# The opening of a two-block transformer forward pass: modulation panels taken in pairs, and the first activations sent through the first up panel chunk by chunk

## What is computed

```python
def modulate(x, shift, scale):
    return x * (1.0 + scale) + shift

def half_ffn(h, shift, scale, gate, wg, wu, wd):
    return h + 0.5 * gate * swiglu(modulate(rms_norm(h), shift, scale), wg, wu, wd)

h = x + grid_pos_embed(n_lat)          # latent tokens, 256 x 1024
hc = ctx                               # context tokens, 256 x 1024
m  = split(silu(c) @ mod_w + mod_b, 9)         # nine vectors of 1024
mc = split(silu(c_ctx) @ mod_w + mod_b, 9)
h  = half_ffn(h,  m[0],  m[1],  m[2],  ffn_w_gate, ffn_w_up, ffn_w_down)
hc = half_ffn(hc, mc[0], mc[1], mc[2], ffn_w_gate, ffn_w_up, ffn_w_down)
```

## Time and profile before

| | us |
|---|---|
| time, median of 3 runs (lowest to highest) | 1908.37 (1902.5 to 1908.42) |
| the profiled execution's own time | 1909.65 |
| its span | 1907.8 |
| TensorE busy in the span | 1850.8 (97%) |
| VectorE busy | 1193.7 (63%) |
| ScalarE busy | 449.5 (24%) |
| GpSimd busy | 531.7 (28%) |
| mean granted TensorE clock | 0.989 of full |

### The profile page before, as it was taken

One profiled execution on the slowest core, in us unless ns is written; L12 is line 12 of the kernel. 1 busy time (PEld: TensorE's weight loads), 2 busy tenths in 40 slices (PEclk: granted clock), 3 DMA queues, 4 the chain that ended last, 5 costly groups with the idle time before them and its releaser, 6 DMA issues.

```text
span 1907.8 us, 32733 instructions
## 1 busy us (share of the span) xinstructions
PE 1850.8 (97%) x13326; PEld 1700.6 (89%) x13326; DVE 1193.7 (63%) x1548; ACT 449.5 (24%) x748; POOL 531.7 (28%) x613
## 2 busy tenths in 40 slices
PE   5999999999999999999999999999999999999999
PEld 2777777887999979999999998999999999899999
DVE  6654543325257987545576976875557796787554
ACT  3100000103121221211135544321112555431110
POOL 1112122121235304343340002553334000244342
PEclk8999999999999999999989999999999999999999
DMA  9325665321333425355544433455454433344552
GB/s 371 119 99 221 259 237 233 133 108 45 111 126 118 160 74 191 145 183 189 179 155 155 155 133 122 144 185 190 177 181 174 169 139 133 133 155 177 185 190 88
DMA packets 44914, 307.35 MB, mean 161 GB/s; under 512 B 5376, under 2 KB 5888, under 8 KB 8320
## 3 DMA queue, kind: packets, MB, share of 16 engines
q1 hardware_dynamic: 40912, 292.66, 42.1%
q10 hardware_dynamic: 3888, 13.03, 1.9%
HBM read 302.53 MB, written 3.15 MB: 160 GB/s over the span
## 4 chain that ended last, share of the span: by engine, by line
PE 87%; DVE 7%; DMA 2%; issue 2%; ACT 1%; SPq 0%; POOL 0%; DVEq 0%; ACTq 0%; POOLq 0%
PE ps L2025 53%; PE ps L2054 23%; DVE wlo L728 2%; DMA landing<-in_stream 1%; DMA ws<-in_stream 1%; PE ps L2536 1%; PE ps L2183 1%; PE ps L2560 1%; PE ps L2546 1%; DVE xlo L795 1%; PE ps L2444 1%; PE ps L2452 1%; PE ps L2510 1%; PE ps L2594 1%; PE ps L2078 1%
## 5 line engine op out<-in xcount | busy, mean ns | idle before, releaser
L728 DVE TENSOR_TENSOR wlo<-landing,whi 128x1024 fp32r<-128x1024 f32 x484 | 610.8, 1297 | 263.7 <-PE ps L2054 171.2
L650 POOL TENSOR_TENSOR whi<-landing,ones 128x16 fp32r<-128x16 f32 x198 | 74.5, 376 | 1355.5 <-PE ps L2025 895.9
L2025 PE MATMUL ps<-xhi,whi 128*128 128x256 f32 (+1 forms) x2368 | 365.8, 306 | 6.4 <-ACT xhi L1691 3.2
L2025 PE MATMUL ps<-xlo,whi 128*128 128x256 f32 (+1 forms) x2368 | 352.4, 301 | 1.1 <-DVE xlo L795 1.1
L2025 PEld LDWEIGHTS ps<-xhi,whi 128*128 128x128 f32 x2368 | 322.6, 193 | 30.1 <-issue 11.8
L2025 PE MATMUL ps<-xhi,wlo 128*128 128x256 f32 (+1 forms) x2368 | 347.0, 299 | 0.5 <-DVE wlo L728 0.5
L2025 PEld LDWEIGHTS ps<-xlo,whi 128*128 128x128 f32 x2368 | 320.9, 193 | 16.4 <-DVE xlo L795 1.5
L2025 PEld LDWEIGHTS ps<-xhi,wlo 128*128 128x128 f32 x2368 | 317.3, 191 | 14.5 <-DVE wlo L728 0.9
L653 POOL TENSOR_SCALAR whi<-landing 128x1024 fp32r<-128x1024 f32 x198 | 230.3, 1163 | 0.0
L652 POOL TENSOR_SCALAR whi<-landing 128x1008 fp32r<-128x1008 f32 x198 | 228.3, 1153 | 0.0
L2054 PE MATMUL ps<-xhi,whi 128*128 128x256 f32 (+1 forms) x1152 | 167.8, 298 | 5.9 <-issue 5.0
(11 more groups left out here) (284 smaller groups left out, 1736.6 us busy)
## 6 DMA issues: line engine op xcount, KB each, us to landing
landing<-in_stream SPq DMA_DIRECT2D x250, 1024.0 KB, 4.8
ws<-in_stream SPq DMA_DIRECT2D x28, 1024.0 KB, 5.0
spectra<-big ACTq DMA_DIRECT2D x8, 256.0 KB, 4.3
ws<-spectra ACTq DMA_DIRECT2D x2, 1024.0 KB, 5.4
ws<-in_tabs ACTq DMA_DIRECT2D x1, 1280.0 KB, 6.1
h<-in_xT ACTq DMA_DIRECT2D x1, 1024.0 KB, 6.3
ws<-in_ctxT ACTq DMA_DIRECT2D x1, 1024.0 KB, 15.2
ws<-in_window ACTq DMA_DIRECT2D x1, 1024.0 KB, 13.6
```

The source lines that it names most:

```text
L650: pool.tensor_tensor(hi[:, 0:FIRST], panel[:, 0:FIRST], ones[:, 0:FIRST], ALU.mult)
L728: ins = v.tensor_tensor(wlo[:, s % 2, c], landing[:, s, c], whi[:, s % 2, c].bitcast(F32), ALU.subtract)
L2025: ins = mm(out, a, b, start=first and opens and k == ks[0], stop=last and k == ks[-1], skip_group_check=True)
```

## The change

The eight lead panels are reordered into four pairs, (0, 4), (1, 5), (2, 6), (3, 7): shift and scale of the same two chunks. Each pair gets its own copy, turn and addition (`pair_copy`, `turn_pair`, `add_pair`), and the addition writes the scale columns straight into `gains`. `first_parts(p)` on VectorE and `first_highs(p)` on ScalarE then make the high and low parts of chunks 2p and 2p+1, and `first_pass(p, ...)` on TensorE runs them through the first up panel, between the lead products. The first up panel gets a buffer of its own (`first_up`) and is loaded behind the second lead panel. The first lead panel is loaded in two halves. The folding of the squares on VectorE is gone, and TensorE adds all eight chunks of squares itself (eight products of 128 x 256 for each token set in place of one). `ctxT` is loaded before `mats`, and `low(G_UP1)`, which stood ahead of `add_mod(0)`, stands behind the last `first_parts`. The core of the diff:

```diff
+        N_PAIR = N_LEAD // 2
+        LEAD = tuple(p + UNROLL * q for p in range(N_PAIR) for q in range(2))
+        first_up = flatc(35, PANEL // T)
+        up0_in = sem("up0_in")
...
-            for g in range(SLOTS):
-                sp.dma_start(landing[:, g], stream[g]).then_inc(landed[g], 16)
+            half = PANEL // 2
+            for n in range(2):
+                c = slice(n * half, (n + 1) * half)
+                sp.dma_start(landing[:, 0, c], stream[0][:, c]).then_inc(landed[0], 16)
+            for g in range(1, SLOTS):
+                sp.dma_start(landing[:, g], stream[LEAD[g]]).then_inc(landed[g], 16)
+                if g == 1:
+                    sp.dma_start(first_up, stream[G_UP1 + N_REST]).then_inc(up0_in, 16)
...
-            for g in (*range(SLOTS, N_LEAD - 1), G_UP1, N_LEAD - 1, *range(G_UP1 + 1, first_rest)):
+            for g in (*range(SLOTS, N_LEAD), *range(G_UP1 + 1, first_rest)):
...
+            def add_pair(p):
+                dve.wait_ge(mod_turned, p + 1)
+                turned = ps[:, 4, 0:16].rearrange("p (c n b) -> p n c b", n=UNROLL, b=2)
...
+                v.tensor_tensor(mcol[:, 2 * p:2 * p + 2, :], turned[:, 0], bias(0), ALU.add).then_inc(mod_added, 1)
+                v.scalar_tensor_tensor(gains[:, 0:2, 2 * p:2 * p + 2].rearrange("p b c -> p c b"), turned[:, 1], 1.0, bias(1),
+                                       ALU.add, ALU.add).then_inc(cols_set, 1)
+            for p in range(N_PAIR):
+                add_pair(p)
+                first_parts(p)
+                if p == 1:
+                    sine_argument(1)
             low(G_UP1, G_UP1 % SLOTS)
-            add_mod(0)
-            add_mod(1)
...
+            pair_copy(0)
+            sine(0)
             log_exp()
             norm_rms(0, 2)
             norm_rms(1, 3)
+            pair_copy(1)
+            first_highs(0)
+            pair_copy(2)
+            first_highs(1)
             sine(1)
-            mod_copy(0)
-            mod_copy(1)
+            pair_copy(3)
+            first_highs(2)
             filter_loads()
-            act.wait_ge(mod_added, 1 + 2)
+            act.wait_ge(mod_added, 1 + N_PAIR)
+            first_highs(3)
...
             def lead(n):
-                pe.wait_ge(landed[n % SLOTS], (n // SLOTS + 1) * 16)
-                mod_product(n, landing[:, n % SLOTS]).then_inc(panel_used, 1)
+                s = n % SLOTS
+                pe.wait_ge(landed[s], (n // SLOTS + (1 if s else 2)) * 16)
+                if n >= 4 and n % 2 == 0:
+                    pe.wait_ge(mod_copied, n // 2 - 1)
+                mod_product(n, landing[:, s], 2).then_inc(panel_used, 1)
...
+            def first_panel(g, s):
+                job = feature(opened_all(up_out(0)), 0, 2 * T)
+                lead(0)
+                lead(1)
+                filter_layer(0)
+                first_sum(0)
+                first_sum(1)
+                turn_pair(0)
+                lead(2)
+                lead(3)
+                turn_pair(1)
+                highs_in(g)
+                first_pass(0, s, job, False)
+                lead(4)
+                first_pass(0, s, job, True)
+                lead(5)
+                turn_pair(2)
+                first_pass(1, s, job, False)
+                filter_layer(1)
+                lead(6)
+                first_pass(1, s, job, True)
+                lead(7)
+                first_pass(2, s, job, False)
+                turn_pair(3)
+                first_pass(2, s, job, True)
+                first_pass(3, s, job, False)
+                first_pass(3, s, job, True).then_inc(hi_used, 1)
+                lows_in(g)
+                return one_pass(wlo, xhi, s, job, last=True)
```

More of the change, by code:

```diff
@@ L643, in high @@
             def high(g, s, turn, n=PANEL):
-                pool.wait_ge(landed[s], (turn + 1) * 16)
+                if isinstance(g, int) and g == G_UP1:
+                    pool.wait_ge(up0_in, 16)
+                    panel = first_up
+                else:
+                    pool.wait_ge(landed[s], (turn + 1) * 16)
+                    panel = landing[:, s]
                 if not isinstance(g, int) or g >= N_LEAD + 2:
@@ L647, in high @@
                     pool.wait_ge(lo_done, g - (N_LEAD + 1))
-                hi, panel = whi[:, s % 2], landing[:, s]
+                hi = whi[:, s % 2]
                 pool.tensor_tensor(hi[:, 0:FIRST], panel[:, 0:FIRST], ones[:, 0:FIRST], ALU.mult)
@@ L727, in low_half @@
                     dve.wait_ge(panel_used, g - 1)
-                ins = v.tensor_tensor(wlo[:, s % 2, c], landing[:, s, c], whi[:, s % 2, c].bitcast(F32), ALU.subtract)
+                panel = first_up if isinstance(g, int) and g == G_UP1 else landing[:, s]
+                ins = v.tensor_tensor(wlo[:, s % 2, c], panel[:, c], whi[:, s % 2, c].bitcast(F32), ALU.subtract)
                 if h2_:
@@ L921, in _ @@
                 last.then_inc(h_set, 1)
[L922 to L929, removed]
+            sine_argument(0)
             for n, src in ((0, h), (1, hc)):
@@ L932, in _ @@
                 v.tensor_tensor(first_norm[:, :, n], src[:] if n == 0 else src, rstd[:, n].unsqueeze(1).to_broadcast([P, KD, T]),
-                                ALU.mult).then_inc(squares_folded, 1)
-            low(G_UP1, G_UP1 % SLOTS)
-            add_mod(0)
-            add_mod(1)
[L937 to L951, removed]
+                                ALU.mult).then_inc(dve_chain, 1)
+                count[0] += 1
+            for p in range(N_PAIR):
[3 more added lines that the diff above has]
+                    sine_argument(1)
+            low(G_UP1, G_UP1 % SLOTS)
             def beside_up1(i):
@@ L1644, in _ @@
             act.dma_start(zfeat, zT).then_inc(hy_in, 16)
+            act.dma_start(ws[:, 0:2048], ctxT).then_inc(ctx_in, 16)
+            act.dma_start(mat[:], mats).then_inc(small_in, 16)
             act.wait_ge(vec_in, 16)
@@ L1648, in _ @@
                          ).then_inc(c_silu, 1)
-            act.dma_start(ws[:, 0:2048], ctxT).then_inc(ctx_in, 16)
             def filter_loads():
@@ L1666, in mod_copy, with pair_copy, first_highs @@
             def mod_copy(i):
-                if i < LEAD_GROUPS:
-                    act.wait_ge(panel_used, UNROLL * (i + 1))
-                else:
-                    act.wait_ge(mod_used, tensor_used(UNROLL * (i + 1 - LEAD_GROUPS) - 1))
+                act.wait_ge(mod_used, tensor_used(UNROLL * (i + 1 - LEAD_GROUPS) - 1))
                 a.activation(mrow[:, i % 2], ps[:, mod_bank(i), 0:COLS], ACT.Identity).then_inc(mod_copied, 1)
-            sine(0)
+            def pair_copy(p):
+                act.wait_ge(panel_used, 2 * (p + 1))
+                a.activation(mrow[:, p % 2], ps[:, mod_bank(p), 0:COLS], ACT.Identity).then_inc(mod_copied, 1)
+            def first_highs(p):
+                for k in (2 * p, 2 * p + 1):
+                    act.wait_ge(norm_scaled, 2 * k + 2)
+                    a.activation(xhi[:, k], first_norm[:, k].rearrange("p n t -> p (n t)"), ACT.Identity).then_inc(norm_hi, 2)
             act.wait_ge(const_set, 3)
@@ L2295, in _, with first_pass @@
-            turn(1)
+                for b in range(4):
+                    pe.wait_ge(sq_done, 4 * n + b + 1)
+                    for k in (2 * b, 2 * b + 1):
+                        last = mm(ps[:, 2 + n, 0:T], ones[:], first_squares[n][:, k * T:(k + 1) * T], start=k == 0, stop=k == KD - 1,
+                                  skip_group_check=True)
+                last.then_inc(sum_done, 1)
+            def first_pass(p, s, job, lo):
+                if lo:
+                    pe.wait_ge(norm_lo, 2 * (2 * p + 2))
+                else:
+                    pe.wait_ge(norm_hi, 2 * (2 * p + 2))
+                return one_pass(whi, xlo if lo else xhi, s, job, ks=(2 * p, 2 * p + 1), first=p == 0 and not lo)
```

102 lines of the change are left out of this document (52 added, 50 removed).

## The result

| | median us | range | runs |
|---|---|---|---|
| before | 1908.42 | 1902.5 to 1909.93 | 9 |
| changed | 1912.13 | 1909.46 to 1915.43 | 9 |

The ratio is 1.0027, 95% interval 1.0016 to 1.0038: 3 to 7 us slower, within the 0.3% that I had called no change. I had forecast 0.7 us less, and the medians differ by 3.7 us the other way. The time lies inside the range, but on the other side of zero. (The ratio follows the means, 1912.3 to 1907.3, and two quick runs of before, 1902.5 and 1903.07, pull its mean down; the medians alone would give 0.19%.)

What follows compares the result with a forecast made beforehand. VectorE was taken to bound the opening from 39 us, after the loads, and TensorE everything from 56.84. The terms put the first up panel's end at 56.1, 0.7 earlier: 1908.37 − 0.7 = 1907.7, range 1901 to 1916.

Steps and rivals of the forecast that it cites:

- The whole question: Opening: when the first up panel ends, 56.84 before; a microsecond there is a microsecond at the end.
- end of the norm: VectorE's norm instructions before the pairs: end at 28.5 (28.1 to 30.1), against about 34.8 before.
- the four pairs: VectorE's additions, scalings and `xlo` for the first up panel: 3.0 us a pair, 12.0 in all.
- three waits: VectorE's waits before pair 1's last `xlo`, the second sine argument and pair 3's addition: 3.0, 1.1 and 1.1 us.
- sine argument, and GpSimd beside: VectorE inside the pairs: second sine argument 2.8 us, plus 1.5 lost to GpSimd's `whi`, expected at pair 2 or 3.
- `wlo`, then the pass: Panel's end: VectorE makes `wlo` behind the last pair, 2.35 us while TensorE waits, then its pass, 3.80.
- the 8 us for the sums: TensorE before the norm: sixteen sum products in place of two take 8 us, ending at about 24.5.
- The rival that they aren't there: Pairs: the waits don't occur, up to 10.5 us earlier, 1897.9; VectorE's floor is 1902.4; chance 0.20.
- the case 0.8 later: Shared port: two whole GpSimd instructions of 1.16 block VectorE, costing 2.3 instead of 1.5 us.
- The clock: Rival: TensorE's clock falls to half between short bursts before the panel's end, giving 1911 to 1920; chance 0.20.
- one of the signs that I had named for a wrong forecast: Profile signs: PEclk 0.50 between 30 and 56, `taps` starting before 53, or TensorE gaining gaps after 57.
- Late loads of panels 6 and 7: Rival: sums delay these loads, issued at about 26 and wanted at 39 and 41; 1909 to 1913; chance 0.04.

Runs made afterwards that it cites:

- e1: Changed kernel with its first lead panel loaded in two parts of 64 whole rows instead of half rows: 1911.94 us, ratio 1.0026.
- e2: Changed kernel with ScalarE's load queue in the old order, `mats` first and `ctxT` behind: 1910.89 us, ratio 1.0014.
- e4: Changed kernel with the first token set's sum products ahead of the first lead and the first sine behind both roots: 1907.95 us, ratio 0.9996.
- e6: Changed kernel with `wlo` of the first up panel made behind the first sine argument, not the last pair: 1911.94 us, ratio 1.0022.
- e7: Changed kernel with the second sine argument behind the last pair and `wlo`, its sine behind the last `xhi`: 1910.76 us, ratio 1.0016.
- e8: Changed kernel with the edits of e1, e4, e5, e6 and e7 together: 1906.91 us, ratio 0.9991.
- e5: Changed kernel with leads 4 and 5 on TensorE ahead of the turn of pair 1: 1908.13 us, ratio 1.0005.
- e10: Changed kernel with six extra products of the squares behind the eighth lead, filling TensorE's pause: 1914.00 us, ratio 1.0036.
- e9: Changed kernel with the edits of e4 and e5 together: 1909.16 us, ratio 1.0005.
- e12: Changed kernel with the edits of e2, e4 and e5 together: 1907.91 us, ratio 0.9999.
- e3: Changed kernel with the edits of e1 and e2 together: 1913.49 us, ratio 1.0027.
- e11: The kernel of e9 with the six extra products of e10: 1908.28 us, ratio 0.9999.

## Why the prediction was wrong

**The whole question is the end of the first up panel: right.** In seven of the profiled executions (changed, e1, e2, e4, e6, e7, e8) the time less the start of `taps` is 1850.9 to 1851.3 us. In the other seven, before among them, it is 1846.4 to 1854.1; one stretch near 1000 us, below, accounts for the three lowest.

**The sum, term by term.** Forecast 56.1, measured 60.8:

| term | forecast | measured |
|---|---|---|
| end of the norm | 28.5 | 32.05 |
| the four pairs | 12.0 | 12.9 (3.14, 3.01, 3.6, 3.16) |
| three waits | 3.0 + 1.1 + 1.1 | 3.09 + 1.00 + 0.83 |
| sine argument, and GpSimd beside | 2.8 + 1.5 | 4.25 |
| `wlo`, then the pass | 2.35 + 3.80 | 2.83 + 3.84 |

**The failed step is the end of the norm**, 3.6 of the 4.7 us. It has two parts. *Loads:* I said that "the first five lead panels and the new buffer" keep "the places of the first six of before", and gave only a date for `ctxT`. I counted the bytes ahead of the lead panels in their own queue and didn't ask what a megabyte moved forward in the other queue takes from them. The first two lead products came 2.9 and 4.3 us later (13.91 and 17.80 against 10.98 and 13.49), and `ctxT` 3.2 us earlier than my 18.3. e2 showed that it is in the main this edit: put back, it gave 1.3 to 2.4 us of the first and 1.4 to 2.5 of the second, depending on which of the five profiles it is held against; why the second stays 1.8 late is open. *TensorE and ScalarE up to the norm:* the 8 us for the sums were right (8.14), and that they and the first sine stand behind the leads and ahead of the roots made them carry the delay: the sums ended at 28.85 instead of 24.5, the sine argument at 24.77. I had written "The VectorE folds they replace are off the path" and costed the products, but not what it means that a product that needs no panel stands behind two that do. e4 put it ahead, and the sine behind the roots, and won 4.2 us. In the four other profiles with this order the norm ended 2.3 to 3.2 us behind the forecast, not 3.6, so the step fails in all of them.

**The waits in the pairs: right in kind**, and in this one profile to 0.3 us; e5 showed that they set the time. That the first fits so well is partly luck: with the clock at half in that loop it was 4.55 to 5.81 in six other profiles. The rival that they aren't there falls. **The pairs** are 0.9 longer: four scalings take 1.38, and in pair 2 ScalarE has the sine (0.42) and the copy (0.37) ahead of its `xhi`.

**GpSimd: right in size, wrong in place.** It met the sine argument, not pair 2 or 3: 1.5 us more there (4.25 against 2.8), as I kept. The Trainium skill (SBUF — State Buffer, Who interferes with whom) says that the engine that issues first has the shared port for its whole instruction and the other blocks. The rows agree: of VectorE's, one of the three L855 took 1.13 instead of 0.42 and L856 1.02 instead of 0.29, and each ended 0.1 to 0.3 us behind a `whi` half. But each came when its `whi` half (1.25 and 1.21 us) was partly done and lost only the rest, 1.4 in the two, so that counting whole GpSimd instructions, as I did for the case 0.8 later, is too much here.

**The clock: there, and cheap in the profile shown** (0.5 us, in which the last low pass outlasted `wlo`; 0.7 by e10's profile). I had written that TensorE's gaps would be at most 2.5 us; the one behind the eighth lead was 3.65, since the sine argument with GpSimd beside it holds pair 2, and PEclk at 0.50 from 50 on is one of the signs that I had named for a wrong forecast. As the whole cause of the loss this rival falls: with the norm early in e4 the loss was gone, though the clock was at half from 27 to 34 and from 48 to 54. As a part of it, it stays open: e10 held the clock up at the end only, and in its profile it was at half in the loop of pair 1, where that costs 1.5 to 2.7 us. **Late loads of panels 6 and 7** and **`filter_loads`: at nothing, right**; leads 6 and 7 and `taps` waited for no landing.

**What the profile alone would have misled about.** `taps` start 4.0 us later, the spans differ by 2.2 and the medians by 3.7. The spans hide 1.8 us, since the clock was down longer near 1000 us in the profile of before (0.51 and 0.81 in the two windows of 10 us from 990 on, against 0.78 and 0.71).

Left open: how often the clock is down in the loop of pair 1 and what that costs in the runs without a profile, why the second lead panel lands 1.8 us late even with the old order of the queue, how much of e4's gain is the sums' place and how much the sine's, and whether the opening can be made faster than before at all. By e9 and e12 that would need the sixth lead panel to land earlier than at 30.

## What to carry to other kernels

Work that needs no load belongs ahead of the work that waits for one, on every engine of the chain; when a reduction is moved from one engine to another, ask first what stands ahead of it in its new queue. Count the bytes of all queues ahead of the first wanted panel, not only of its own. And before adding two gains, look for the wait at which both end: here each was worth 4 us and both together 3.

## What the runs showed of the hardware

**A second place where the clock falls.** Far from the change, near 1000 us, eleven of the fourteen profiled executions lose about 4.5 us at a lower clock, though TensorE is busy for 9.2 to 10 of each 10 us. The changed kernel, and then e9 (columns as in the first windows above):

```profile
990.00:1000.00 10.00, 9.18 (x61) 8.95 (x60) 9.96 (x14) 3.35 (x11) 4.68 (x4) 0.78 0.49 196
1000.00:1010.00 10.00, 10.00 (x64) 10.00 (x64) 3.55 (x6) 2.63 (x4) 1.38 (x2) 0.71 0.56 211
```

```profile
990.00:1000.00 10.00, 9.18 (x79) 9.09 (x80) 9.93 (x15) 3.99 (x13) 5.30 (x4) 1.00 0.44 153
1000.00:1010.00 10.00, 10.00 (x85) 10.00 (x85) 7.51 (x9) 4.99 (x5) 0.00 (x0) 1.00 0.75 283
```

In 20 us 164 matmuls were done at the full clock, and 125 with the fall. In e3, e9 and e12, where it is missing, the time less the start of `taps` is 1846.4 to 1846.7, some 4.5 less than in the seven others. The same gap stands in the runs: of 34 of the kernel before in one session 3 lie at 1902.3 to 1903.6 and the other 31 at 1906.3 to 1910.9. That these are the runs without the fall is an inference; only three profiles show it. For a change worth 4 us this is the larger noise, and the reason for timing each kernel in many runs. What makes the clock fall there no run shows.

**The clock at the very start.** With sums on TensorE from 8.36 on (e4) the leads at 14.49 and 17.48 took 1.07 us each; in the changed kernel, where TensorE had done nothing until 13.91, those at 13.91 and 17.80 took 1.93. The profile's column of the granted clock reads 1.00 in both, so that this is the clock is an inference from the durations: 1.93 is what a lead takes where the column reads 0.50, as in e10 above. Work given to an idle TensorE ahead of the first panel nearly halved the time of the leads behind it (in e4, e8, e9, e11 and e12).
